# The fourth group of pooled sums in a hybrid decoder step, in five pieces between the issues of value pages

## Chip, cores and metric

The kernel runs on one core of a Trainium2 chip. The metric is the device time of one launch in microseconds (us). A core has a matrix engine (TensorE, PE in the rows; its weight loads are PEld), a vector engine (VectorE, DVE), a scalar engine (ScalarE, ACT), GpSimd (POOL) and a fifth (SyncE, SP) that only issues transfers. Each works through its own list of instructions in order, and they meet by semaphores. An engine's sequencer is marked with a q (POOLq).

## What is computed

Two layers of a decoder trunk, over 256 prompt tokens and 8 sequences of 8 sample tokens (320 columns). Each layer mixes by three kinds of heads, then runs a gated feed-forward part:

```python
h   = rms_norm(x, norm1[l]);  proj = h @ w_in[l]
q, k, v, z, xbc, dt_raw, xp = jnp.split(proj, SPLITS, axis=-1)
o_sb   = stick_breaking_attention(q, k_all, v_all, ...)   # sample tokens read 2048 cached positions, in pages of 128
y_ssd  = ...                                              # chunked state-space scan, 16 heads, and new states
y_pool = multiscale_pool(xp, pool_hist, ...)
x = x + jnp.concatenate([o_sb, y_ssd, y_pool], axis=-1) @ w_out[l]
x = x + (jax.nn.silu(g_c) * u) @ w_down[l]

def multiscale_pool(...):                                 # 4 groups of 128 channels, windows 2, 4, 8, 16
    for g, win in enumerate(POOL_WINDOWS):
        wsum = sum of the last `win` rows of group g
        pooled.append(wsum / count)
    diff = pooled - xp
    y = einsum('blgc,gcd->blgd', diff, pool_w) * pool_scale
```

## The kernel before

Channels lie on partitions, tokens along the free axis. The large products (w_in, w_out, w_gate, w_up, w_down) stream weights in units, split each into a high and a low part and run three matmuls for each tile; they fill most of the time. Between w_in and w_out of each layer lies the **mix stage**, about 320 to 615 us after the start in layer 0 and about 1965 to 2255 us in layer 1. All that changes lies there.

The mix stage is written out by hand as 152 **slots**, numbered 8*qn + k. Every engine has its own loop over the slots, and does in each what belongs to it. In slot s TensorE transposes a page of cached keys (`key_page`, L1332), multiplies a page of cached values by attention weights (`value_page`, L1376, from slot 16 on), in some slots computes scores of a half chunk (`chunk_z`, L1344), and then does the step that the table `MIX` names for the slot: ("pool", g) is the product of group g's pooled difference with pool_w (L1473; groups 0 to 3 in slots 27, 28, 29 and 39), ("c", blk, j) are sums for the scan (L1421; for block 1 in slots 30 to 33), ("n", h) is a part of the new prompt state (L1453; slots 34 and 36) which reads the tile `xw`.

Value pages lie in a ring of 8 (`vring`). GpSimd issues them: in slot s, from 16 on, `value_in` waits until TensorE has used the page that lies in place s mod 8, reads the page's number into a register (L582, a TENSOR_LOAD and two register operations), computes an address (L583, MOVE) and issues the transfer (L583, DMA_DIRECT2D, 256 KB). The page issued in slot s is the one that TensorE needs in slot s + 8. The first eight pages are issued ahead of slot 0.

Behind the issue of its slot GpSimd does other work, also in order: `pooled(g)` for groups 0 to 3 in slots 1, 6, 9 and 20; `gate(blk)` in slots 18 and 41 (L641 to L645, with two drains); `weighted_x(blk)`, which writes `xw` (L616), in slots 5, 28 and 46. `pooled(g)` adds a row of sums to itself, shifted, g + 1 times (L595), so that the window doubles each time, from `xp` into `p1`, from `p1` into `p2` and back; behind each sum stands `pool.drain()` (L596), which holds GpSimd's sequencer until what it issued is done. Then come the means and differences (L599 to L608, drains L602 and L606), and the last of them releases TensorE's ("pool", g) through `p_diff`. ("n", 0) waits for `xw` of block 1 through `blk_xw`.

Of the kernel before, what the change touches and what calls it, by code (L numbers as in the profile page):

```python
# [20 lines left out]
ALU = mybir.AluOpType  # L21
# [31 lines left out]
WINS = (2, 4, 8, 16)  # L53
# [73 lines left out]
def build(nc, a, o):  # L127

    with ExitStack() as ctx:
# [11 lines left out]
        def sb(name, shape, dt=F32):  # L141
            off = at[0]
            at[0] += (size(shape) + 31) // 32 * 32
            return sb_at(name, shape, dt, off)
# [49 lines left out]
        XPL = SEQ + PH + NB * (NT + PH)  # L194
        xp = sb("xp", [P, PLT, XPL])
# [212 lines left out]
        def read(eng, l, *step):  # L408

            b, n = USE[step]  # L410
            eng.wait_ge(mix_read[b], l * USES[b] + (n + 1))
# [119 lines left out]
        def _(pool):  # L531
# [30 lines left out]
            for l in range(DEPTH):  # L562
# [14 lines left out]
                def value_in(q, k):  # L577

                    if q:
                        pool.wait_ge(v_used, l * (CHUNKS * 8) + (8 * (q - 1) + k + 1))  # L580
                    at_page = (q // 4 * 2 + k // 4) * PAGES + 4 * (3 - q % 4) + k % 4
                    page = pool.value_load(pages[0:1, at_page:at_page + 1], min_val=0, max_val=a["cache_v"].shape[1] - 1)  # L582
                    pool.dma_start(vring[:, k, :], a["cache_v"][l, page].rearrange("s h d -> s (h d)")  # L583
                                   ).then_inc(v_loaded[k], 16)

                xps = xp[:, :, SEQ + PH:].rearrange("p g (b t) -> p g b t", b=NB)

                def pooled(g):

                    win = WINS[g]  # L590
                    src, w, bufs = xp[:, g, :], 1, [p1, p2]
                    while w < win:
                        dst = bufs[0][:]
                        bufs.reverse()
                        pool.tensor_tensor(dst[:, 2 * w - 1:], src[:, 2 * w - 1:], src[:, w - 1:XPL - w], ALU.add)  # L595
                        pool.drain()  # L596
                        src, w = dst, 2 * w
                    news = pdiff[:, g, SEQ:TOK].rearrange("p (b t) -> p b t", b=NB)
                    pool.tensor_scalar(pdiff[:, g, 0:SEQ], src[:, PH:PH + SEQ], 1.0 / win, None, ALU.mult)  # L599
                    pool.tensor_scalar(news, src[:, SEQ + PH:].rearrange("p (b t) -> p b t", b=NB)[:, :, PH:], 1.0 / win,  # L600
                                       None, ALU.mult)
                    pool.drain()  # L602

                    pool.tensor_tensor(pdiff[:, g, 0:16], src[:, PH:PH + 16], con[:, K_CNT + 16 * g:K_CNT + 16 * g + 16],
                                       ALU.mult)
                    pool.drain()  # L606
                    pool.tensor_tensor(pdiff[:, g, 0:SEQ], pdiff[:, g, 0:SEQ], xp[:, g, PH:PH + SEQ], ALU.subtract)
                    pool.tensor_tensor(news, news, xps[:, g, :, PH:], ALU.subtract).then_inc(p_diff, 1)  # L608

                def weighted_x(blk):  # L610

                    T = tokens(blk)[1]
                    pool.wait_ge(blk_exp, l * 3 + blk + 1)
                    if blk == 0:
                        read(pool, l, "dec")
                    pool.tensor_tensor(xw[0:T, :].rearrange("p (h d) -> p h d", h=SSH),  # L616
                                       xtok[0:T, 0:SSW].rearrange("p (h d) -> p h d", h=SSH),
                                       tk[0:T, 3, :].unsqueeze(2).broadcast_to([T, SSH, DH]), ALU.mult
                                       ).then_inc(blk_xw, 1)

                def conv_tails_out():
                    read(pool, l, "ctail", 1)
                    read(pool, l, "ctail", 2)
                    pool.dma_start(o["new_ssm_conv_prompt"][l, 0], ctail[0:3, :]).then_inc(conv_stored, 16)
                    pool.dma_start(o["new_ssm_conv_sample"][l].rearrange("b k c -> (b k) c"), ctail[3:27, :]
                                   ).then_inc(conv_stored, 16)
                    pool.dma_start(poolw[:], a["pool_w"][l].rearrange("g c d -> c g d")).then_inc(poolw_loaded, 16)

                def pool_tails_out():
                    read(pool, l, "ptail", 0)  # L630
                    read(pool, l, "ptail", 1)
                    pool.dma_start(o["new_pool_prompt"][l, 0], ptailP[:]).then_inc(tail_stored, 16)
                    pool.dma_start(o["new_pool_sample"][l].rearrange("b k c -> (b k) c"), ptail[0:NB * PH, :]
                                   ).then_inc(tail_stored, 16)

                def gate(blk):

                    cols = slice(blk * P, (blk + 1) * P)
                    read(pool, l, "y", blk, 2)
                    read(pool, l, "y", blk, 3)  # L640
                    pool.tensor_tensor(y[:, :, cols], y[:, :, cols], z[:, :, cols], ALU.mult)  # L641
                    pool.drain()
                    pool.tensor_tensor(z[:, :, cols], y[:, :, cols], y[:, :, cols], ALU.mult)
                    pool.drain()
                    pool.tensor_tensor(z[:, 0:4, cols], z[:, 0:4, cols], z[:, 4:8, cols], ALU.add).then_inc(y_sq, 1)  # L645

                def state_decay(i):

                    s_old = s_seq[i % 4]
                    written(pool, l, "T", i, 0)  # L650
                    written(pool, l, "T", i, 1)
                    pool.tensor_tensor(s_old[:], s_old[:], dec[:, :, 2 + i:3 + i].broadcast_to([P, SST, NS]), ALU.mult
                                       ).then_inc(s_decayed, 1)

                def state_rows(i):

                    if i >= 2:
                        written(pool, l, "N", i - 2, 1)
                    elif i == 0:
                        written(pool, l, "y", 2, 3)  # L660
                    pool.tensor_scalar(bm[:, i % 2, :], xtok[0:SAMP, SSW:], con[0:SAMP, K_SEQ + i:K_SEQ + i + 1], None,
                                       ALU.mult).then_inc(s_bm, 1)

                def state_out(i):
                    read(pool, l, "N", i, 0)
                    read(pool, l, "N", i, 1)
                    pool.dma_start(o["new_ssm_sample"][l, i].rearrange("(j e) p n -> (e p) j n", e=2), s_seq[i % 4][:]
                                   ).then_inc(s_stored[i % 4], 16)
# [5 lines left out]
                for qn in range(CHUNKS + 3):  # L674
                    for k in range(8):
                        slot = 8 * qn + k
                        if 2 <= qn <= CHUNKS:
                            value_in(qn - 1, k)
                        if slot in (1, 6, 9, 20):
                            pooled((1, 6, 9, 20).index(slot))  # L680
                        for blk in range(3):
                            if slot == SLOT["cum", blk] + 2:
                                weighted_x(blk)
                        if slot == SLOT["ctail", 2] + 1:
                            conv_tails_out()
                        if slot == SLOT["ptail", 1] + 1:
                            pool_tails_out()
                        for blk in range(2):
                            if slot == SLOT["y", blk, 3] + 1:
                                gate(blk)  # L690
                        if slot == SLOT["n", 1] + 1:
                            read(pool, l, "n", 0)
                            read(pool, l, "n", 1)
                            pool.dma_start(o["new_ssm_prompt"][l, 0].rearrange("(j e) p n -> (e p) j n", e=2), snew[:]
                                           ).then_inc(snew_stored, 16)
                        for i in range(NB):
                            if slot == SLOT["N", i, 1] + 1:
                                state_out(i)
                            if slot == SLOT["T", i, 1] + 1:
                                state_rows(i)  # L700
                                state_decay(i)
# [29 lines left out]
                n = KT // 2 if l + 1 < DEPTH else KT // 2 - 1  # L731
# [352 lines left out]
        def _(pe):  # L1084
            def products(l, base, n, planes, half=8, between=None, ready=None, side=None, swap=0,
# [38 lines left out]
                if n > 1:  # L1124
                    with pe.Fori(1 if between else 0, n) as i:
                        one(i + base)

            DOWN = [down for _, down in B_PART]
            def norm_sum(n):

# [1193 lines left out]
```

## Time and profile before

| | |
|---|---|
| time, median of 3 runs (lowest, highest) | 3336.67 us (3335.12, 3338.84) |
| the profiled execution: its time, its span | 3336.89 us, 3334.1 us |
| busy: PE, PEld, DVE, ACT, POOL | 96%, 91%, 57%, 40%, 12% of the span |
| mean granted clock of TensorE | 0.982 of full speed |
| chain that ended last, by engine | PE 90%, issue 2%, ACT 2%, POOLq 2%, POOL 1%, DMA 1%, DVE 1% |

The span is that of the traced instructions, from the first to the last; the execution's own time is 2.8 us longer. "Chain that ended last" follows the program back from its last instruction, at each step to what released it. "issue" is time in which an engine waited for nothing that the profile shows. The idle time of an engine counts only where the chain goes through it.

### The profile page before, as it was taken

The page shows a single profiled execution, that of the slowest core. Times are in us where ns is not written, and L with a number is a line of the kernel's source. Part 1 is how long each engine was busy: PE and PEld are TensorE (multiplying, and loading weights), DVE is VectorE, ACT ScalarE, POOL GpSimd, SP SyncE. Part 2 cuts the span into 40 slices and gives each one's busy share as a digit, 9 for nine tenths or more (in the row PEclk, how much of TensorE's full clock was granted, in tenths as well). Part 3 has the DMA queues.
Part 4 walks back from the last instruction along what each step waited for, and adds up shares of the span by engine and source line. Part 5 has one row for each costly group of instructions (what it writes and reads, how often), then busy time and mean ns, then how long its engine had stood idle before and what let it go on. Part 6 is the DMA issues. An engine that isn't in the chain of part 4 may idle for free.

```text
span 3334.1 us, 62446 instructions
## 1 busy us (share of the span) xinstructions
PE 3217.1 (96%) x23776; PEld 3025.9 (91%) x23776; DVE 1902.7 (57%) x3339; ACT 1348.0 (40%) x1663; POOL 408.7 (12%) x513
## 2 busy tenths in 40 slices
PE   7999899899999999999999998989999999999998
PEld 7999566699999999999999985658999999999998
DVE  4574655466653666456656655454666546654664
ACT  4553555434433333333335545563444333333332
POOL 0000654220000000000200025531100000000002
PEclk9999898899999999999999999999999999999999
DMA  6443698644444444444444447985444444444443
GB/s 186 139 127 107 213 304 282 219 151 151 147 145 151 149 146 148 151 156 142 150 143 130 135 132 227 322 288 172 150 151 149 143 151 151 144 149 150 151 145 103
DMA packets 469098, 554.37 MB, mean 166 GB/s; under 512 B 20635, under 2 KB 414444, under 8 KB 468788
## 3 DMA queue, kind: packets, MB, share of 16 engines
q1 hardware_dynamic: 440275, 466.93, 44.1%
q0 software_dynamic: 26192, 84.73, 7.9%
q8 instruction: 114, 1.87, 0.2%
q10 hardware_dynamic: 2449, 0.27, 0.1%
q14 instruction: 68, 0.56, 0.1%
HBM read 535.50 MB, written 16.38 MB: 166 GB/s over the span
## 4 chain that ended last, share of the span: by engine, by line
PE 90%; issue 2%; ACT 2%; POOLq 2%; POOL 1%; DMA 1%; DVE 1%; ACTq 0%; DVEq 0%
PE ps L1107 26%; PE ps L1108 26%; PE ps L1109 26%; PE ps L1332 2%; PE ps L1376 2%; PE ps L1344 1%; PE ps L1494 1%; PE ps L1484 1%; POOLq L596 1%; DMA vring<-in_cache_v 1%; PE ps L1478 1%; POOLq L582 0%; PE ps L1421 0%; ACT wz L934 0%; PE ps L1358 0%
## 5 line engine op out<-in xcount | busy, mean ns | idle before, releaser
L1579 DVE TENSOR_TENSOR wl<-raw,wh 128x1024 fp32r<-128x1024 f32 (+1 forms) x752 | 924.6, 1239 | 1027.2 <-ACT wh L746 1020.4
L746 ACT ACTIVATE wh<-raw 128x1024 fp32r<-128x1024 f32 (+1 forms) x752 | 781.5, 1041 | 1637.4 <-PE ps L1109 1635.0
L1107 PE MATMUL ps<-fh,wh 128*128 128x320 f32 x2816 | 870.6, 309 | 0.0
L1109 PE MATMUL ps<-fh,wl 128*128 128x320 f32 x2816 | 870.1, 309 | 0.0
L1108 PE MATMUL ps<-fl,wh 128*128 128x320 f32 x2816 | 870.1, 309 | 0.0
L1107 PEld LDWEIGHTS ps<-fh,wh 128*128 128x128 f32 x2816 | 528.5, 188 | 0.2
L1108 PEld LDWEIGHTS ps<-fl,wh 128*128 128x128 f32 x2816 | 528.5, 188 | 0.2
L1109 PEld LDWEIGHTS ps<-fh,wl 128*128 128x128 f32 x2816 | 528.5, 188 | 0.0
L1107 PE MATMUL ps<-hh,wh 128*128 128x320 f32 x1408 | 438.4, 311 | 5.5 <-DVE wl L1579 4.5
L1107 PE MATMUL ps<-ah,wh 128*128 128x320 f32 x1408 | 437.1, 310 | 0.0
L1109 PE MATMUL ps<-hh,wl 128*128 128x320 f32 x1408 | 436.2, 310 | 0.0
L1109 PE MATMUL ps<-ah,wl 128*128 128x320 f32 x1408 | 435.1, 309 | 0.0
L1108 PE MATMUL ps<-hl,wh 128*128 128x320 f32 x1344 | 416.4, 310 | 0.0
L1108 PE MATMUL ps<-al,wh 128*128 128x320 f32 x1344 | 415.2, 309 | 0.0
L1107 PEld LDWEIGHTS ps<-hh,wh 128*128 128x128 f32 x1408 | 265.4, 188 | 7.6 <-issue 5.0
L1107 PEld LDWEIGHTS ps<-ah,wh 128*128 128x128 f32 x1408 | 264.3, 188 | 1.6 <-issue 0.3
L1109 PEld LDWEIGHTS ps<-hh,wl 128*128 128x128 f32 x1408 | 265.3, 188 | 0.0
L1109 PEld LDWEIGHTS ps<-ah,wl 128*128 128x128 f32 x1408 | 264.3, 188 | 0.0
L1108 PEld LDWEIGHTS ps<-hl,wh 128*128 128x128 f32 x1344 | 253.3, 188 | 0.0
L1108 PEld LDWEIGHTS ps<-al,wh 128*128 128x128 f32 x1344 | 252.3, 188 | 0.0
L722 POOL DMA_DIRECT2D out_new_ffn_conv_prompt<-ftail x6 | 3.1, 523 | 1612.0 <-DVE ftail L1671 1612.0
L1332 PE MATMUL ps<-con,kring 128*128 128x128 f32 x1024 | 167.9, 288 | 7.6 <-ACT kT L910 6.9
(355 smaller groups left out, 3572.1 us busy)
## 6 DMA issues: line engine op xcount, KB each, us to landing
raw<-in_w_gate SPq DMA_DIRECT2D x88, 1024.0 KB, 5.1
raw<-in_w_up SPq DMA_DIRECT2D x88, 1024.0 KB, 5.1
raw<-in_w_in SPq DMA_DIRECT2D x72, 1024.0 KB, 5.2
kring<-in_cache_k SPq DMA_DIRECT2D x256, 256.0 KB, 4.0
vring<-in_cache_v POOLq DMA_DIRECT2D x256, 256.0 KB, 4.6
raw<-in_w_down SPq DMA_DIRECT2D x64, 1024.0 KB, 5.4
raw<-in_w_out SPq DMA_DIRECT2D x32, 1024.0 KB, 5.5
raw<-in_w_down SPq DMA_DIRECT2D x32, 768.0 KB, 4.6
```

Source lines behind the costliest of these rows:

```text
L596: pool.drain()
L746: act.activation(wh[:, s % 2, half, :], raw[:, s, half, :], ACT.Copy).then_inc(hi_done, 1)
L1107: pe.matmul(out, wh[:, s % 2, kk, w], hi(row), start=first, stop=False)
L1108: pe.matmul(out, wh[:, s % 2, kk, w], lo(row), start=False, stop=False)
L1109: mm = pe.matmul(out, wl[:, s % 2, kk, w], hi(row), start=False, stop=last)
L1332: mm = pe.transpose(ps[4 + n % 2][:, j * P:(j + 1) * P], kring[:, k, j * P:(j + 1) * P], ident)
L1344: mm = pe.matmul(ps[q % 2][32 * j:32 * j + 32, :], qp[:, q // 4, bb, j, :], kT[bb][:, j, :], start=(bb == 0), stop=(bb == 1))
L1376: mm = pe.matmul(ps[6][32 * j:32 * j + 32, 0:P], wz[:, k // 4, k % 4, j, :], vring[:, k, j * P:(j + 1) * P], start=False, stop=last)
L1478: mm = pe.transpose(bank[:, j * P:(j + 1) * P], s_seq[i % 4][:, 4 * h + j, :], ident)
L1484: mm = pe.matmul(bank[:, j * 16:(j + 1) * 16].rearrange("p (e t) -> p e t", e=2), sT[:, i % 2, j * P:(j + 1) * P], csS[:, 2 * j:2 * j + 2, ...
L1494: mm = pe.matmul(bank[:, j * NS:(j + 1) * NS], xw[0:SAMP, (4 * h + j) * P:(4 * h + j + 1) * P], bm[:, i % 2, h * NS:(h + 1) * NS], start=T ...
L1579: dve.tensor_tensor(wl[:, s % 2, half, :], raw[:, s, half, :], wh[:, s % 2, half, :].bitcast(F32), ALU.subtract).then_inc(lo_done, 1)
```

## The change

The function `pooled(g)` is taken apart into `pooled_sum(g, n)`, one doubling with its drain, and `pooled_mean(g)`, the rest. Groups 0 to 2 are still made in one go in slots 1, 6 and 9. Group 3, which was made whole in slot 20, is now made in five pieces: its four sums in slots 22, 23, 24 and 25 and its mean in slot 26, each behind the issue of that slot's value page.

```diff
-                def pooled(g):
-                    win = WINS[g]
-                    src, w, bufs = xp[:, g, :], 1, [p1, p2]
-                    while w < win:
-                        dst = bufs[0][:]
-                        bufs.reverse()
-                        pool.tensor_tensor(dst[:, 2 * w - 1:], src[:, 2 * w - 1:], src[:, w - 1:XPL - w], ALU.add)
-                        pool.drain()
-                        src, w = dst, 2 * w
+                def pooled_sum(g, n):
+                    w = 2 ** n
+                    src = (p2, p1)[n % 2][:] if n else xp[:, g, :]
+                    dst = (p1, p2)[n % 2][:]
+                    pool.tensor_tensor(dst[:, 2 * w - 1:], src[:, 2 * w - 1:], src[:, w - 1:XPL - w], ALU.add)
+                    pool.drain()
+
+                def pooled_mean(g):
+                    win, src = WINS[g], (p1, p2)[g % 2][:]
...
                        if 2 <= qn <= CHUNKS:
                            value_in(qn - 1, k)
-                        if slot in (1, 6, 9, 20):
-                            pooled((1, 6, 9, 20).index(slot))
+                        for g, at_ in enumerate((1, 6, 9)):
+                            if slot == at_:
+                                for n in range(g + 1):
+                                    pooled_sum(g, n)
+                                pooled_mean(g)
+                        if 22 <= slot < 26:
+                            pooled_sum(3, slot - 22)
+                        if slot == 26:
+                            pooled_mean(3)
```

The lists of TensorE, VectorE, ScalarE and SyncE stay as they were. On GpSimd, in layer 0, this stood around slot 20 before; the first row is the issue of slot 20's page, the last one begins that of slot 21's (`pages` holds the page numbers, `p_0_150` and `p_0_151` are `p1` and `p2`; drains are not listed, and stand where the code has them):

```order
L583 DMA vring<-in_cache_v 128x512
L595 TENSOR_TENSOR p_0_150<-xp 128x454
L595 TENSOR_TENSOR p_0_151<-p_0_150 128x452
L595 TENSOR_TENSOR p_0_150<-p_0_151 128x448
L595 TENSOR_TENSOR p_0_151<-p_0_150 128x440
L599 TENSOR_SCALAR pdiff_152<-p_0_151 128x256
L600 TENSOR_SCALAR pdiff_152<-p_0_151 128x64
L604 TENSOR_TENSOR pdiff_152<-p_0_151,con 128x16
L607 TENSOR_TENSOR pdiff_152<-pdiff_152,xp 128x256
L608 TENSOR_TENSOR pdiff_152<-pdiff_152,xp 128x64
L582 TENSOR_LOAD pages
```

The nine compute instructions have left this place, and the issue of slot 21 follows that of slot 20 at once. In the changed kernel this stands in slots 22 to 24, from the issue of slot 22's page to that of slot 24's (the sum is on line 593 there):

```order
L583 DMA vring<-in_cache_v 128x512
L593 TENSOR_TENSOR p_0_150<-xp 128x454
L582 TENSOR_LOAD pages
L582 ISA x2
L583 ISA
L583 DMA vring<-in_cache_v 128x512
L593 TENSOR_TENSOR p_0_151<-p_0_150 128x452
L582 TENSOR_LOAD pages
L582 ISA x2
L583 ISA
L583 DMA vring<-in_cache_v 128x512
```

Each sum, and the drain behind it, now stands between two issues. Behind slot 26 the mean ends like this, with the issues of slots 27 and 28 and then the tile `xw` (`xw_134`, line 617 there):

```order
L608 TENSOR_TENSOR pdiff_152<-pdiff_152,xp 128x256
L609 TENSOR_TENSOR pdiff_152<-pdiff_152,xp 128x64
L582 TENSOR_LOAD pages
L582 ISA x2
L583 ISA
L583 DMA vring<-in_cache_v 128x512
L582 TENSOR_LOAD pages
L582 ISA x2
L583 ISA
L583 DMA vring<-in_cache_v 128x512
L617 TENSOR_TENSOR xw_134<-xtok,tk 128x1024
```

Before, the issues of eight pages (slots 21 to 28) stood between the group's last instruction and `xw`; now two do. The number of instructions and of drains (six for the group) is the same.

## Rows read from the trace of the kernel before

**Rows 1.** TensorE in order of time, layer 0: start, us, engine, line, operation, tiles

```profile
382.26 0.81 PE L1473 MATMUL ps<-pdiff,poolw 128*128 128x320 f32 x2
382.91 0.60 PE L1332 MATMUL ps<-con,kring 128*128 128x128 f32 x4
392.24 0.66 PE L1376 MATMUL ps<-vring,wz 128*32 128x128 f32 x8 [8.73 <-DMA vring<-in_cache_v]
392.67 1.94 PE L1344 MATMUL ps<-kT,qp 128*32 128x512 f32 x8
394.53 1.22 PE L1473 MATMUL ps<-pdiff,poolw 128*128 128x320 f32 x2
...
396.11 0.43 PE L1376 MATMUL ps<-vring,wz 128*32 128x128 f32 x8
...
402.86 1.04 PE L1344 MATMUL ps<-kT,qp 128*32 128x512 f32 x8
...
405.36 0.43 PE L1376 MATMUL ps<-vring,wz 128*32 128x128 f32 x8
405.71 1.16 PE L1453 MATMUL ps<-xtok,xw 128*128 128x128 f32 x8
```

**Rows 2.** The same view in layer 1, the same slot

```profile
2036.53 0.66 PE L1376 MATMUL ps<-vring,wz 128*32 128x128 f32 x8 [8.61 <-DMA vring<-in_cache_v]
```

**Rows 3.** GpSimd in order of time, layer 0, slots 20 to 28; brackets: idle before

```profile
378.14 0.55 POOL L583 DMA_DIRECT2D vring<-in_cache_v  x1 [0.59 <-issue]
378.70 0.95 POOL L595 TENSOR_TENSOR p<-xp 128x454 f32<-128x454 f32 x1
382.08 3.27 POOL L595 TENSOR_TENSOR p<-p 128x452 f32<-128x452 f32 x3 [2.43 <-issue]
385.52 1.57 POOL L599 TENSOR_SCALAR pdiff<-p 128x256 f32<-128x256 f32 x1 [0.17 <-issue]
...
388.04 0.72 POOL L607 TENSOR_TENSOR pdiff<-pdiff,xp 128x256 f32<-128x256 f32 x1
...
389.25 0.59 POOL L583 DMA_DIRECT2D vring<-in_cache_v  x1 [0.21 <-issue]
390.42 0.54 POOL L583 DMA_DIRECT2D vring<-in_cache_v  x1 [0.57 <-issue]
...
397.69 0.54 POOL L583 DMA_DIRECT2D vring<-in_cache_v  x1 [0.62 <-issue]
398.24 1.92 POOL L616 TENSOR_TENSOR xw<-xtok,tk 128x1024 f32<-128x1024 f32 x1
```

**Rows 4.** Busy us by engine in stretches (PE, PEld, DVE, ACT, POOL), granted clock, DMA

```profile
383.00:392.00 9.00, 0.51 (x5) 0.27 (x3) 3.09 (x4) 1.01 (x3) 6.79 (x11) 0.62 0.32 91
392.00:396.00 4.00, 3.76 (x22) 1.69 (x22) 0.00 (x0) 0.22 (x1) 1.71 (x4) 0.58 0.75 213
```

**Rows 5.** The drain behind the first sum at 378.14: its ns (min/median/max), its start

```profile
L596 POOLq DRAIN  x1: 3854/3854/3854, 378.1 to 378.1; - x1
```

**Rows 6.** GpSimd in order of time: other work that follows a drain close behind an issue

```profile
344.60 1.33 POOL L599 TENSOR_SCALAR pdiff<-p 128x256 f32<-128x256 f32 x1 [3.16 <-issue]
...
422.27 0.54 POOL L583 DMA_DIRECT2D vring<-in_cache_v  x1 [1.46 <-issue]
...
427.47 1.89 POOL L643 TENSOR_TENSOR z<-y 128x1024 f32<-128x1024 f32 x1 [2.27 <-issue]
...
2026.50 3.27 POOL L595 TENSOR_TENSOR p<-p 128x452 f32<-128x452 f32 x3 [2.85 <-issue]
...
2071.93 1.89 POOL L643 TENSOR_TENSOR z<-y 128x1024 f32<-128x1024 f32 x1 [1.97 <-issue]
```

**Rows 7.** Page transfers: count, KB, median us to landing; page at 378.14, then 389 to 398

```profile
vring<-in_cache_v POOLq DMA_DIRECT2D x1, 256.0 KB, 3.7
...
vring<-in_cache_v POOLq DMA_DIRECT2D x8, 256.0 KB, 3.2
```

**Rows 8.** The means' first instruction over the whole run: ns, min/median/max

```profile
L599 POOL TENSOR_SCALAR pdiff<-p x8: 847/856/2078, 344.6 to 2029.9; 128x256 f32<-128x256 f32 x8
```

## The prediction, on record before the changed kernel ran

> **What bounds the kernel now.** I read the page first: TensorE is busy nearly all the time, and the chain that ended last gives GpSimd's sequencer and GpSimd itself a few per cent. So the change can only matter where the chain leaves TensorE inside the mix stage. I asked TensorE's own order of time there, looking for brackets. One wait stands out: it was ready for slot 29's value page at 383.51 (392.24 less 8.73) and waited 8.73 us for a transfer [rows 1]; layer 1 shows the same wait of 8.61 us at the same slot [rows 2]. Then GpSimd's order of time: slot 20's page was issued at 378.14, then all of group 3 ran, and slot 21's page, which is the one that slot 29 needs, went out at 389.25 [rows 3]; it landed some 3 us later. The wait is therefore GpSimd's delay of the issue, 11.1 us from one issue to the next where two issues that follow at once are 1.17 apart (389.25 to 390.42).
>
> Behind the wait TensorE ran slowly for a while: the granted clock was 0.62 and 0.58 in these stretches [rows 4], on its way to the lower of its levels, 1.2 instead of 2.4 GHz. The same three steps took 0.66, 1.94 and 1.22 us where they take 0.43, 1.04 and 0.81 otherwise [rows 1]: 1.54 us lost. The spot costs about 8.7 + 1.5 = 10.2 us a layer, 20 us in the run. That is the most the change can win.
>
> **What the change does, part by part.**
>
> *Removed: the block in slot 20.* Slot 21's page goes out at 378.14 + 1.17 = 379.31, lands by 382.5, and slot 29 starts at 383.5 without a wait. Slot 22's page goes out at 380.48. With its clock kept, TensorE would reach slot 30 at 383.5 + (396.11 - 392.24) - 1.54 = 385.8, that is 10.28 us ahead of before, and everything behind it by as much if nothing new is late: ("n", 0) of slot 34, at 405.71 before [rows 1], at 395.43.
>
> *Added: a drain behind each of five issues.* This is the term that decides. The same number of drains runs, but before only the first of them stood right behind an issue. Its length was 3854 ns [rows 5] for a sum of 0.95 us: the sum ended at 379.65, and the next one could start only 2.43 us later; the three sums behind it, with no new issue between, took 3.27 us together, no gap worth counting [rows 3]. Wherever a drain follows an issue this gap is there: 3.16, 2.27, 2.85 and 1.97 us [rows 6]; in the order of time I found no case without it, and 0.1 to 0.2 us where no transfer had been issued since the last drain. The drain at 378.14 ended at 382.0 and the page issued at 378.14 landed 3.7 us after issue [rows 7], at 381.9, so my reading is that the drain also waits for the transfer that GpSimd has just issued. So the extra is paid once a block before, and five times now.
>
> The size for each. The two long brackets (3.16, and 2.43 and 2.85 in this very place) follow pages issued 1.2 us apart; 2.27 and 1.97 follow pages about 2 us apart (422.27 with 1.46 idle before it) [rows 6], which is closer to the new order. I take 2.85 for the piece in slot 22, which follows four issues in a row, and 2.1 for the other four. From the end of a drain to the next issue 1.2 us pass (388.04 to 389.25: register load, address, issue) [rows 3]. So:
> - slot 22: issue 380.48; 0.56 (issue) + 0.95 (sum) + 2.85 + 1.2 = 5.56: slot 23's issue at 386.04.
> - slots 23, 24, 25: 0.56 + 0.95 + 2.1 + 1.2 = 4.81 each: slot 26's issue at 400.47.
> - slot 26: the mean from L599 to the next issue took 389.25 - 385.52 = 3.73 us, of which L599 had 1.57 where its median is 0.86 [rows 3, 8]; TensorE's neighbours are quieter now, so 3.73 - 0.71 = 3.02. With issue and gap 0.56 + 3.02 + 2.0 (0.1 of the gap is in the 3.02 already) = 5.58: slot 27 at 406.05, slot 28 at 407.22.
> - `xw` behind it: 407.22 + 0.55 + 1.92 [rows 3] = 409.69.
>
> *TensorE against this.* Slot 34's value page is that of slot 26: issued at 400.47, landed some 3.1 us later [rows 7] at 403.6, where TensorE would want it at 405.36 - 10.28 = 395.1. So 8.5 us of waits lie on the value pages of slots 31 to 34, about 2 us each. Then ("n", 0), which had 5.5 us to spare before (`xw` ended at 400.16, TensorE came at 405.71 [rows 1, 3]), is reached at 403.9 and waits 5.8 us for `xw`. Sum 14.3 for 10.28 saved: ("n", 0) starts 4.0 us later than before. VectorE and ScalarE wait for TensorE here, so nothing hides it, and behind slot 34 the pages are ahead again (GpSimd issues one in 1.17 us, TensorE needs one in about 2). In this tangle of waits its clock will fall again in part; I charge half of the 1.54: 0.7 us, where 0 and 1.54 are the bounds. Sum 4.7 us a layer, less 0.2 for VectorE and ScalarE having run ahead: 4.5, twice 9.0.
>
> Made against the profiled execution, 3336.9 us (its span of 3334.1 and 2.8 around it; 0.2 above the median of the runs): 3336.9 + 9.0 = 3346 us.
>
> **Bounds of the unknown.** The gap at 3.16 throughout gives 4 x 1.06 + 0.31 = 4.6 us more a layer and full clock loss 0.8: 10 a layer, 3357. If a drain only waits for the landing of one lone page, 2.9 to 3.2 us after issue [rows 2, 3, 7] and no more, the gap is about 1.5 for the sums and 1.2 for the mean, and the layer comes out 4.0 - 1.3 - 3 x 0.6 - 0.9 = 0.0, with clock 0 to 1: 3337 to 3339. The Trainium skill, "DMA: Bandwidth & Descriptors", section "Anatomy of one DMA", gives a transfer by GpSimd as 2.0 us + bytes / 436 GB/s, an estimate of 2.6 us for a page; by that alone the pieces would come still closer, and the time would be about 3335. The rows show 3.2 and 3.7, so the page's figure is low here, under the load of the key pages.
>
> **Rivals.**
> - *Pieces fit between the issues* (the other side). If the gap belonged to the first drain after the long gate of slot 18, or to a train of issues, and not to each issue, a slot with a piece takes 0.56 + 0.95 + 0.1 + 1.2 = 2.8 us: slot 26's issue at 391.7, `xw` done at 391.7 + 3.7 + 1.2 + 2.5 = 399.1; no page is late by more than a few tenths, ("n", 0) starts at 399.1 instead of 405.7. 6.6 us a layer, and no clock lost: 3323 us. It decides from a mean gap of about 1.35 us downwards: there the new order starts to win. For it speaks only that no drain of before stood behind one lone issue after a pause of 5 us; against it all brackets of [rows 3, 6], whose smallest is 1.97. 9 in 100.
> - *Landing is all that counts*: as worked out in the bounds, 3337 to 3343, no measurable change. For it: the drain of [rows 5] ended 0.1 us behind the landing. Against it: at 422.27 the multiplication of 2.38 us covers most of the landing and still 2.27 were left. 22 in 100.
> - *Forecast*: gap near 2.1 to 2.9, slower. 69 in 100.
>
> **How the numbers follow.** Within 0.2% (6.7 us, about what a measurement of this kernel can tell from no change) is 3330 to 3343.3. The forecast's own range is 3342 to 3355; with the landing rival it begins at 3338, and the 9 in 100 of the fitting pieces and a few above stay out. Slower by over 0.2%: 0.69. Same: 0.22. Faster: 0.09.
>
> **What would show each step.** In the changed kernel's GpSimd order: slots 22 to 26 issued 4.5 to 5.6 us apart, each drain there 3.4 to 4.3 us long, against 2.8 us apart under the first rival. In TensorE's: no wait at slot 29; brackets of 1 to 3 us on the value pages of slots 31 to 34; a wait of 5 to 6 us at ("n", 0) that is put down to GpSimd's `xw`; a granted clock below 1 somewhere between 388 and 412. If `xw` ends before 405.7 the forecast is wrong in its sign; if the pieces are 4.8 us apart and the time still doesn't rise, then ("n", 0) was not where it binds, and I have missed work that hides it.

## The result and the profile after

The changed kernel takes 3343.03 us (median of 10 runs, 3336.82 to 3348.22); the kernel before, run beside it on the same chip, 3335.0 us (10 runs, 3329.73 to 3339.55). The ratio is 1.0022 with an interval of 1.0012 to 1.0032: slower, by 4 to 11 us. The profiled execution took 3342.78 us, its span 3340.4 us, its mean granted clock is 0.980. Line numbers of the kernel after are 8 higher than before on TensorE.

TensorE in layer 0, the kernel after, in order of time (answers to [rows 1]); brackets are idle time and what ended it:

```profile
382.98 0.43 PE L1384 MATMUL ps<-vring,wz 128*32 128x128 f32 x8
385.36 0.43 PE L1384 MATMUL ps<-vring,wz 128*32 128x128 f32 x8
...
387.80 0.42 PE L1384 MATMUL ps<-vring,wz 128*32 128x128 f32 x8 [0.48 <-DMA vring<-in_cache_v]
388.76 1.16 PE L1429 MATMUL ps<-con,tk 128*128 128x128 f32 x8 [0.54 <-DVE pool_lo L2066]
...
392.41 0.43 PE L1384 MATMUL ps<-vring,wz 128*32 128x128 f32 x8 [1.61 <-DMA vring<-in_cache_v]
...
396.63 0.43 PE L1384 MATMUL ps<-vring,wz 128*32 128x128 f32 x8 [2.28 <-DMA vring<-in_cache_v]
396.88 1.47 PE L1352 MATMUL ps<-kT,qp 128*32 128x512 f32 x8
398.28 2.08 PE L1429 MATMUL ps<-con,tk 128*128 128x128 f32 x8
...
401.27 0.42 PE L1384 MATMUL ps<-vring,wz 128*32 128x128 f32 x8 [0.22 <-DMA vring<-in_cache_v]
406.92 2.05 PE L1461 MATMUL ps<-xtok,xw 128*128 128x128 f32 x8 [5.22 <-POOL xw L617]
```

The 8.73 us at slot 29 are gone (382.98 has no bracket). In their place stand four short waits on the value pages of slots 31 to 34, 4.59 us together, 0.54 us for VectorE between them, and 5.22 us at ("n", 0), which are put down to GpSimd's `xw`. The same in layer 1 (answers to [rows 2]); slot 33 lies between with 0.79 us:

```profile
2033.78 0.43 PE L1384 MATMUL ps<-vring,wz 128*32 128x128 f32 x8 [1.16 <-DMA vring<-in_cache_v]
2038.10 0.65 PE L1384 MATMUL ps<-vring,wz 128*32 128x128 f32 x8 [0.55 <-DMA vring<-in_cache_v]
...
2047.28 0.42 PE L1384 MATMUL ps<-vring,wz 128*32 128x128 f32 x8 [0.39 <-DMA vring<-in_cache_v]
2053.01 2.04 PE L1461 MATMUL ps<-xtok,xw 128*128 128x128 f32 x8 [5.31 <-POOL xw L617]
```

GpSimd after, layer 0, slots 19 to 28 (answers to [rows 3]):

```profile
375.06 0.58 POOL L583 DMA_DIRECT2D vring<-in_cache_v  x1
...
378.54 0.54 POOL L583 DMA_DIRECT2D vring<-in_cache_v  x1 [0.62 <-issue]
379.09 0.95 POOL L593 TENSOR_TENSOR p<-xp 128x454 f32<-128x454 f32 x1
384.82 0.55 POOL L583 DMA_DIRECT2D vring<-in_cache_v  x1 [4.77 <-issue]
385.38 0.95 POOL L593 TENSOR_TENSOR p<-p 128x452 f32<-128x452 f32 x1
389.06 0.54 POOL L583 DMA_DIRECT2D vring<-in_cache_v  x1 [2.73 <-PE ps L1384]
...
393.56 0.55 POOL L583 DMA_DIRECT2D vring<-in_cache_v  x1 [3.00 <-PE ps L1384]
...
398.21 0.54 POOL L583 DMA_DIRECT2D vring<-in_cache_v  x1 [2.95 <-issue]
...
404.30 0.54 POOL L583 DMA_DIRECT2D vring<-in_cache_v  x1 [0.60 <-issue]
404.86 1.91 POOL L617 TENSOR_TENSOR xw<-xtok,tk 128x1024 f32<-128x1024 f32 x1
```

The issues of slots 22 to 26 stand 6.28, 4.24, 4.50 and 4.65 us apart, and slot 27's follows 4.91 us later (layer 1: 6.58, 4.31, 4.20, 4.39 and 5.58). "<-PE ps L1384" names the semaphore event that came last, TensorE's release of a place in the ring. That release isn't the cause: the place that slot 24's page goes into was free since TensorE's slot 24, before 378, and the issue came at 389.06. GpSimd was held by its drain. The drains show it, one by one (their ns, min/median/max, and start; answers to [rows 5]; the fifth is the first one of the mean):

```profile
L594 POOLq DRAIN  x1: 5052/5052/5052, 378.6 to 378.6; - x1
L594 POOLq DRAIN  x1: 3016/3016/3016, 384.8 to 384.8; - x1
L594 POOLq DRAIN  x1: 3276/3276/3276, 389.1 to 389.1; - x1
L594 POOLq DRAIN  x1: 3097/3097/3097, 393.6 to 393.6; - x1
L603 POOLq DRAIN  x1: 3039/3039/3039, 398.3 to 398.3; - x1
```

And the pages issued at 378.54, 384.82 and 389.06, right ahead of the first three (median us from issue to landing; answers to [rows 7]; those of 393.56 and 398.21 took 3.0 each):

```profile
vring<-in_cache_v POOLq DMA_DIRECT2D x1, 256.0 KB, 4.8
vring<-in_cache_v POOLq DMA_DIRECT2D x1, 256.0 KB, 2.9
vring<-in_cache_v POOLq DMA_DIRECT2D x1, 256.0 KB, 3.2
```

384.82 + 2.9 = 387.7, and the drain ended at 384.8 + 3.0 = 387.8; 378.54 + 4.8 = 383.3, and the drain ended at 378.6 + 5.05 = 383.7. Each of these drains ends with the landing of the page ahead of it, 0.1 to 0.4 us behind.

TensorE's clock (answers to [rows 4]; columns as there):

```profile
396.00:401.00 5.00, 4.37 (x28) 2.91 (x28) 1.06 (x3) 0.44 (x1) 1.75 (x3) 0.66 0.45 111
401.00:407.00 6.00, 0.56 (x10) 0.27 (x9) 1.30 (x3) 5.36 (x10) 4.83 (x7) 0.77 0.47 131
407.00:411.00 4.00, 4.00 (x26) 3.28 (x28) 1.99 (x6) 0.00 (x0) 2.42 (x5) 0.50 0.63 217
```

It fell twice, in the stretch behind the waits of slots 32 and 33, and to the lower level behind the wait at ("n", 0): that step took 2.05 us for the 1.16 of [rows 1].

To measure the whole place free of the rest of the program I take the time from TensorE's cum product in slot 26 to the one in slot 44. Before, in layer 0:

```profile
377.30 0.40 PE L1413 MATMUL ps<-tk,con 128*128 128x16 f32 x2
...
425.97 0.28 PE L1413 MATMUL ps<-tk,con 64*64 64x16 f32 x2
```

That is 48.67 us (layer 1: 48.0). After it is 50.58 (378.22 to 428.80) and 50.81 (2023.71 to 2074.52): 1.91 and 2.82 us longer, 4.7 together. Call this the **cost of the place**. It rests on one trace of each kernel: e4 below has the code of before in all these slots, and in its trace the place took 47.75 and 47.41 us, 1.5 us less in all. So differences of 1 to 2 us in this measure tell nothing.

### The profile page after: what moved, and what is told of

Read it like the earlier page. It is cut to its first block, busy times and chain, and to the rows that moved or that the text cites. A ratio compares the mean times of both kernels' runs of the same rounds, so it can differ in the third digit from the quotient of the medians.

```text
span 3340.4 us, 62446 instructions
## 1 busy us (share of the span) xinstructions
PE 3223.8 (97%) x23776; PEld 3033.6 (91%) x23776; DVE 1901.4 (57%) x3339; ACT 1347.7 (40%) x1663; POOL 408.7 (12%) x513
## 4 chain that ended last, share of the span: by engine, by line
PE 91%; issue 2%; ACT 2%; DVE 2%; POOLq 1%; POOL 0%; ACTq 0%; DVEq 0%; DMA 0%
PE ps L1115 26%; PE ps L1116 26%; PE ps L1117 26%; PE ps L1340 2%; PE ps L1384 2%; PE ps L1352 1%; PE ps L1502 1%; PE ps L1492 1%; PE ps L1486 1%; PE ps L1366 0%; PE ps L1429 0%; ACT wz L942 0%; PE ps L1250 0%; DVE sq L1978 0%; PE ps L1158 0%
```

## The experiments

Ten kernels ran in three groups, each group beside the kernel before. "Cost of the place" is against the trace of before, layer 0 + layer 1; negative is faster. "By ratio" is (ratio - 1) times 3335 us, with its interval.

| kernel | cost of the place, us | ratio | by ratio, us |
|---|---|---|---|
| the change | 1.9 + 2.8 = 4.7 | 1.0022 (1.0012, 1.0032) | 7 (4, 11) |
| e1, pieces with semaphores | -10.2 - 9.6 = -19.8 | 0.994 (0.9924, 0.9957) | -20 (-25, -14) |
| e2, block in slot 22 | -1.9 - 2.8 = -4.7 | 0.9983 (0.9972, 0.9994) | -6 (-9, -2) |
| e3, one more drain in slot 27 | 5.2 + 5.6 = 10.8 | 1.0042 (1.0027, 1.0056) | 14 (9, 19) |
| e4, before, drains only behind the place | -0.9 - 0.6 = -1.5 | 1.0064 (1.0048, 1.008) | 21 (16, 27) |
| e5, block in slot 30 | -9.4 - 5.4 = -14.8 | 0.9964 (0.995, 0.9977) | -12 (-17, -8) |
| e6, before, block with semaphores | -3.7 - 3.8 = -7.5 | 0.9986 (0.9972, 0.9999) | -5 (-9, 0) |
| e7, pieces in slots 30 to 34 | -2.3 + 3.0 = 0.7 | 1.0005 (0.9992, 1.0019) | 2 (-3, 6) |
| e8, drains of the sums doubled | 2.0 + 1.6 = 3.6 | 1.0027 (1.0014, 1.004) | 9 (5, 13) |
| e9, no drain in the whole mix stage | -8.4 - 7.5 = -15.9 | 0.9957 (0.9943, 0.9971) | -14 (-19, -10) |
| e10, `xw` ahead of the mean | 1.0 + 0.9 = 1.9 | 1.0014 (1.0, 1.0027) | 5 (0, 9) |

**e1: the same five pieces, without drains.** The changed kernel with each step chained to the next by a semaphore.

```diff
-                    pool.tensor_tensor(dst[:, 2 * w - 1:], src[:, 2 * w - 1:], src[:, w - 1:XPL - w], ALU.add)
-                    pool.drain()
+                        if n:
+                            pool.wait_ge(p_sum, l * 7 + n)
+                        pool.tensor_tensor(dst[:, 2 * w - 1:], src[:, 2 * w - 1:], src[:, w - 1:XPL - w], ALU.add
+                                           ).then_inc(p_sum, 1)
```

> The changed kernel, with group 3's pieces in the same slots 22 to 26, but chained by a semaphore (each sum counts it up, the next piece waits for it) instead of by drains; nothing is left out. Theory (a drain also waits for the page that GpSimd has just issued, 2 to 3 us beyond the sum): without drains the slots with a piece are 1.7 to 2 us apart (0.55 issue, 0.95 sum, 0.2), not 4.2 to 6.3; no page is late, xw is ready before TensorE comes to (n, 0), the wait of 8.7 us at slot 29 is gone and nothing takes its place: about 10 us a layer, ratio to before 0.994 (3315 us). Rival (work of any kind behind each issue is what costs, whatever closes it): spacing stays over 4 us and the time at 1.002 of before.

Measured: 0.994, as expected, 27 us below the change. GpSimd in order of time, slots 22 to 24 (the issues go on at 381.70 and 383.33):

```profile
377.38 0.54 POOL L584 DMA_DIRECT2D vring<-in_cache_v  x1 [0.61 <-issue]
377.93 0.96 POOL L621 TENSOR_TENSOR p<-xp 128x454 f32<-128x454 f32 x1
378.81 0.55 POOL L584 DMA_DIRECT2D vring<-in_cache_v  x1
379.38 0.95 POOL L621 TENSOR_TENSOR p<-p 128x452 f32<-128x452 f32 x1
380.26 0.55 POOL L584 DMA_DIRECT2D vring<-in_cache_v  x1
```

The first three sums take 1.44 us of GpSimd each with their issue, barely more than the 1.17 of an issue alone; the next page's issue follows the sum without a gap, so its register load and address are worked off while the sum runs. `xw` ends at 390.6, and TensorE has two waits left up to slot 34, 0.97 for VectorE and 0.91 for ScalarE. So the pieces, their slots and their arithmetic are not what costs. The drains are.

**e2: the whole group in slot 22.** The change's code undone, the block of before moved by two slots.

```diff
-                        if slot in (1, 6, 9, 20):
-                            pooled((1, 6, 9, 20).index(slot))
+                        if slot in (1, 6, 9, 22):
+                            pooled((1, 6, 9, 22).index(slot))
```

> The kernel before with one number changed: the whole of group 3 in slot 22 instead of 20, with its drains. Theory (each drain close behind an issue pays 2 to 3 us, so the number of such drains counts): one such drain as before, so the block takes 10.6 us; page 23 goes out some 11 us after page 22, TensorE waits about 7 us at slot 31 instead of 8.7 at slot 29, xw is in time. Ratio 0.999 to 1.000, 1 to 4 us faster than before. Rival (the place costs: work in slots 22 to 26 stands too close ahead of xw): as slow as the change, ratio 1.002, with a wait of several us at (n, 0).

Measured: 0.9983, a little better than expected. GpSimd spends 11.9 us from slot 22's issue to slot 23's, and TensorE has one wait for it, at slot 31 (6.96 us in layer 1):

```profile
393.67 0.65 PE L1376 MATMUL ps<-vring,wz 128*32 128x128 f32 x8 [6.49 <-DMA vring<-in_cache_v]
```

and not at ("n", 0), since `xw` ends at 399.3. So the later slots are not what costs. In one go the group pays for one landing there and wins 5 to 6 us on before; in five goes it pays for five and loses 5 to 7.

**e3: one drain more.** The change, and a bare drain behind slot 27's issue, with nothing to wait for but that page.

```diff
+                        if slot == 27:
+                            pool.drain()
```

> The changed kernel with one bare drain more in each layer, behind the issue of slot 27's page, with no compute instruction ahead of it in that slot. Theory: the drain waits until that page has landed, 3.0 to 3.3 us from the issue; slot 28's issue and xw come 3.1 us later, (n, 0) too: 6 us more than the change, ratio to before about 1.004. Rival (the extra belongs to a drain behind a compute instruction, not to the transfer): under 0.1 us a drain, ratio as of the change, 1.002.

Measured: 1.0042. The added drain of layer 0 (ns, start) and what TensorE waits for `xw` now, where it waited 5.22:

```profile
L690 POOLq DRAIN  x1: 3290/3290/3290, 403.5 to 403.5; - x1
```

```profile
410.63 0.77 PE L1463 MATMUL ps<-xtok,xw 128*128 128x128 f32 x2 [8.54 <-POOL xw L617]
```

The last step of the mean ended at 403.55, so no GpSimd work was under way, and the drain lasted 3.29 us; its page landed 3.2 us after issue. All of it comes out at ("n", 0): 8.54 - 5.22 = 3.32 us. The price of a drain behind a fresh page is measured by itself here, and it reaches the time in full (3.3 and 2.8 us of the place, by layer).

**e4: bare drains where I thought there was cover.** The kernel before, with drains in slots 50, 54, 58 and 62.

```diff
+                        if slot in (50, 54, 58, 62):
+                            pool.drain()
```

> The kernel before with a bare drain behind the issues of slots 50, 54, 58 and 62 of each layer, where GpSimd has nothing else to do and is up to 8 slots ahead. It is to measure the drain itself against the landing of the page issued just ahead. Theory: each of the 8 drains lasts 3 to 5 us and ends 0.1 to 0.6 us after the landing; the time stays (ratio 1.000), since the lead covers it. Rival (a drain costs a fixed 2 us after an issue, whenever the page lands): lengths all near 2 us and not in step with the landings.

Measured: 1.0064. A miss on the time, which was to stay at 1.000. The drains ended with the landings as was said, but lasted longer, 3.4 to 6.8 us over both layers, for the pages landed later here. That of slot 58 (its ns and start, and its page's landing in us):

```profile
L682 POOLq DRAIN  x1: 6810/6810/6810, 460.0 to 460.0; - x1
```

```profile
vring<-in_cache_v POOLq DMA_DIRECT2D x1, 256.0 KB, 6.6
```

Behind it in the same slot GpSimd makes the tile `bm`, which TensorE needs in slot 60 for the sample states, and TensorE waits 9.84 us (9.44 in layer 1):

```profile
467.93 2.05 PE L1496 MATMUL ps<-bm,xw 64*128 64x128 f32 x8 [9.84 <-issue]
```

I had looked only at the eight slots of lead that value pages have. A drain holds back all that stands behind it on GpSimd, and the tile with the least lead decides.

**e5: the whole group in slot 30.** The block with its drains, in two tiles of its own, behind `xw` in the program.

```diff
-                        if 22 <= slot < 26:
-                            pooled_sum(3, slot - 22)
-                        if slot == 26:
-                            pooled_mean(3)
+                        if slot == 30:
+                            for n in range(4):
+                                pooled_sum(3, n)
+                            pooled_mean(3)
```

> Group 3 made whole, with its six drains, behind the issue of slot 30's page, in two tiles of its own. Theory (a drain costs the landing of the page issued just before it, once for a block, and what counts is whether TensorE has that much lead over the issues and whether the block stands ahead of xw): GpSimd is some 11 to 12 us in the block; the issues have about 10 us of lead by then and xw of slot 28 is done before it, so TensorE waits at most 2 to 3 us on the page for slot 39 and not at (n, 0); ratio about 0.994 to 0.996 to the kernel before, near the 0.994 of the pieces chained by semaphores. Rival (the number of drains or the place in a page train sets the time wherever the group stands): a wait of 6 to 9 us shows up at slot 38 or 39 and the ratio is 0.998 to 1.000.

Measured: 0.9964. The first drain lasted 5.79 us and slot 31's page went out at 403.05, 13.7 us after slot 30's, longer than expected, and yet TensorE waited for no page behind it, and at most 1 us for anything between slots 30 and 40. TensorE came to slot 39, which needs the page issued at 403.05, at 406.64: one landing, in a block, is covered there. In layer 1 it had 2.19 and 0.52 us of page waits in slots 27 and 28, ahead of the block; they are not its doing.

**e6: the kernel before without the group's drains.** Group 3 whole in slot 20, its steps chained by semaphores as in e1.

> The kernel before, with group 3 whole in slot 20, each of its steps chained to the next by a semaphore instead of a drain. Theory (of the 11.1 us from issue to issue about 2.5 are the first drain waiting for the page's landing, the rest is work): the issues of slots 20 and 21 stand 8 to 8.8 us apart, TensorE's wait at slot 29 shrinks from 8.7 to 5.5 to 6.5 us, ratio 0.998 to 0.999. Rival (the wait comes from the block being in slot 20 at all, the drains only mark work that takes as long anyway): 11 us apart, wait 8.7, ratio 1.000.

Measured: 0.9986, the theory's value, though its interval reaches 0.9999. The block, issue to issue, and the wait that it leaves:

```profile
376.07 0.55 POOL L584 DMA_DIRECT2D vring<-in_cache_v  x1 [0.59 <-issue]
376.63 0.95 POOL L620 TENSOR_TENSOR p<-xp 128x454 f32<-128x454 f32 x1
377.67 3.14 POOL L620 TENSOR_TENSOR p<-p 128x452 f32<-128x452 f32 x3
...
383.72 0.59 POOL L584 DMA_DIRECT2D vring<-in_cache_v  x1
```

```profile
387.25 0.65 PE L1405 MATMUL ps<-vring,wz 128*32 128x128 f32 x8 [4.90 <-DMA vring<-in_cache_v]
```

7.65 us for the 11.1 of before: the gap of 2.43 us behind the first sum [rows 3] is 0.09, and 1.1 us more is saved on other steps. Of that, 0.7 us is the mean's first instruction, which took 0.85 us here and 1.57 in the trace of before, and isn't shown to be the drains' doing. Expected were 8 to 8.8 and a wait of 5.5 to 6.5; it is 4.90 and 4.47, which is 3.8 and 4.1 less than before. So the one drain behind the fresh page accounts for 2.3 us of the wait, and more than half of the wait was the work standing all in one slot.

**e7: the five pieces in slots 30 to 34.** As e5, but in pieces with their drains.

> The five pieces with their drains in slots 30 to 34 (two tiles of their own), behind xw instead of ahead of it. Theory (each piece costs its page's landing wherever it stands, and the price shows at the first thing TensorE needs of GpSimd): issues 4.2 to 4.8 us apart again, group 3 done some 22 us after the issue of slot 30's page; now the product of group 3 in slot 39 waits for it, 6 to 9 us, and there is no wait at (n, 0). Ratio 0.999 to 1.000, about 12 us above the whole block in slot 30. Rival (the damage of the change came from standing ahead of xw, and later pieces are free): no wait over 2 us, ratio 0.996 like the whole block there.

Measured: 1.0005, and 14 us above e5. The issues stand 4.3 to 6.0 us apart once more, and the wait is where group 3 is first needed:

```profile
414.23 1.41 PE L1486 MATMUL ps<-pdiff,poolw 128*128 128x320 f32 x2 [6.23 <-POOL pdiff L614]
```

(9.67 us in layer 1.) Later slots don't make the pieces cheap. Each pays its landing there too.

**e8: the drains of the sums doubled.**

```diff
                         if 22 <= slot < 26:
                             pooled_sum(3, slot - 22)
+                            pool.drain()
```

> The changed kernel with a second drain right behind the drain of each of the four sums. Theory (a drain waits for the landing of what GpSimd issued, and has nothing left to wait for the second time): second drains of under 0.1 us, issues 4.2 to 6.3 us apart as in the changed kernel, ratio 1.002. Rival (each drain costs a fixed couple of us in this neighbourhood): 2 us more a slot, waits of 8 us more a layer, ratio 1.007 or more.

Measured: 1.0027, the change's within the intervals. The eight added drains:

```profile
L687 POOLq DRAIN  x8: 41/41/41, 383.5 to 2041.0; - x8
```

41 ns each. A drain costs next to nothing by itself; what costs is the issue between one and the next.

**e9: no drain at all in the mix stage.** e1, with semaphores also in groups 0 to 2 and in the gates.

> Pieces in slots 22 to 26 as in the change, with semaphores in place of every drain of GpSimd in the mix stage, those of groups 0 to 2 and of the gates too. Theory (only drains behind a fresh page whose page TensorE then waits for cost anything, and those of group 3 were the only such): same as with group 3's alone chained, 0.994, or up to 3 us better (0.993). Rival (drains of the other groups and gates cost too): another 5 us or more, ratio 0.992 or below.

Measured: 0.9957, no better than e1, whose interval it overlaps. The rival's 0.992 or below lies outside its interval: it falls. Whether the other drains cost a little stays open, since e9 has a loss of its own. TensorE waits 2.21 and 2.32 us for VectorE's `pool_lo` at the step of slot 31 (0.97 us in layer 0 of e1) and runs slower behind it. Ahead of that `pool_lo` VectorE's scan took 2.52 us for 1.28 in e1:

```profile
386.11 2.52 DVE L1980 TENSOR_TENSOR_SCAN sq<-rz,sq,lq 128x512 f32<-128x512 f32 x1
```

GpSimd, earlier here, was computing `xw` at the same time (385.62 to 387.54). Layer 1 shows the same, 2.63 us beside `xw`. That the two hold each other up is a reading of these rows; no run tests it.

**e10: `xw` taken ahead of the mean.** The change, with `weighted_x(1)` in slot 26 ahead of `pooled_mean(3)` (group 3 in tiles of its own).

> The changed kernel, its pieces with their drains in slots 22 to 26, but xw is computed in slot 26 ahead of the mean instead of in slot 28 behind it (group 3 sums in two tiles of its own, since p1 and p2 lie under the tile that TensorE's next step lets be written). Theory (5.2 us of the change's loss stand at (n, 0), which waits for xw): xw ends some 6 us earlier, near 401, and the wait at (n, 0) is gone; slot 27's page goes out 2 us later, so slot 35's value page waits 3 to 4 us instead; net 1 to 2 us a layer and some clock won back, ratio 0.9995 to 1.0015. Rival (xw is not what binds, the issues are): as much waiting behind as was won, ratio 1.002.

Measured: 1.0014, inside the theory's range, though not told apart from the change's 1.0022 by the ratios, so the rival (1.002) isn't excluded. `xw` ends at 401.0, there is no wait at ("n", 0), and slot 35's value page takes its place:

```profile
408.53 0.66 PE L1390 MATMUL ps<-vring,wz 128*32 128x128 f32 x8 [5.07 <-DMA vring<-in_cache_v]
```

(4.17 in layer 1; 3 to 4 were expected.) With 3.8 us of work between slot 26's issue and the first drain of the mean, the step behind that drain started after 0.23 us idle, for 1.30 in the change: work between an issue and the drain covers the landing. But moving `xw` passes most of the lateness on, since GpSimd as a whole is late by then.

## Why the prediction came out as it did

The forecast was slower, 3346 in 3338 to 3355, by drains that wait for a page each; measured were 3343.0. The mechanism is the one that was forecast. The size is less sure: 3343.0 lies just inside the 3343.3 up to which the prediction would have called it no change, while the ratio, 1.0022, lies just outside 0.2%. Point by point:

- *The wait at slot 29 goes, and 10.28 us with it.* Right, and somewhat more. Slot 30's page step begins at 385.36 for 396.11, and slot 26's cum product 0.92 later than before (378.22 for 377.30): 11.7 us won. The prediction missed two brackets: before, the page steps of slots 27 and 28 had waited as well, 0.95 and 0.46 us, for pages that were issued at 376.96 and 378.14, behind the drain in slot 18's gate. Both pages went out ahead of group 3's block, so the change didn't remove these 1.4 us: e4, with the code of before, has a single wait of 0.33 us there.

```profile
379.85 0.43 PE L1376 MATMUL ps<-vring,wz 128*32 128x128 f32 x8 [0.95 <-DMA vring<-in_cache_v]
...
381.91 0.42 PE L1376 MATMUL ps<-vring,wz 128*32 128x128 f32 x8 [0.46 <-DMA vring<-in_cache_v]
```

- *Each drain behind a fresh issue waits for the landing.* Right: shown by the five drains of the change, by e3 (nothing else to wait for), by e1 (no drains, no gaps) and by e8 (second drains 41 ns). One reading against the rival "landing is all that counts" was too quick. At 422.27 the multiplication of 2.38 us was said to cover most of the landing; that page took 4.2 us, so 1.3 of the 2.27 us of gap were landing. About 0.8 us were not, and at 2067.03 (page landed after 3.2 us, drain 4.74 us long) 1.5 us were neither landing nor computing. What such a drain behind slot 41's gate waits for besides is open.
- *The size of the gap, 2.85 and 2.1 us.* Spacings of 5.56, then 4.81 three times, then 5.58 were foreseen; they are 6.28, 4.24, 4.50, 4.65 and 4.91. Sum 25.57 against 24.58, 1.0 us less. The drains were to last 3.4 to 4.3 us; they lasted 5.05 behind the train and 3.0 to 3.3 else. The first piece was under-priced by 0.7, the other four over-priced by 0.4 on average; that the sum came out so close is in part luck, for the two errors work against each other. The second rival's rule, lone pages land in 2.9 to 3.2 us and a drain waits for just that, is the better rule for the lone ones; it erred on the page of slot 22, the last of four in a row, with 4.8. Its sum, 3337 to 3339, came out too low by that page and by the full clock loss. The estimate of 2.6 us for a page by the Trainium skill ("DMA: Bandwidth & Descriptors", "Anatomy of one DMA") is low by 0.3 to 0.6 us for the lone pages of layer 0 here, and by 4 us for the page of slot 58 in e4.
- *When the pieces start.* This is the term that was mis-sized most. Slot 22's issue was put at 380.48 and came at 378.54, 1.9 us earlier in the run and 2.9 earlier against TensorE. I had carried over the time of slot 20's issue from one execution [rows 3]. GpSimd was ahead well before that, in code that is the same in both kernels: slot 18's page went out at 365.18 after and at 367.69 before. The drain in slot 18's gate, behind that page, even took some of this back (6.48 us long for 5.85; it ended at 371.7 for 373.7). Why GpSimd runs earlier in the one execution is open. `xw` was done at 406.8 and not at 409.7, 1.9 us by the start and 1.0 by the spacings. In layer 1, the same sum from slot 20's issue at 2022.14 puts slot 22's at 2024.48; it came at 2024.16, 0.3 us earlier in the run and 1.3 against TensorE.
- *The waits behind.* 8.5 us on value pages and 5.8 at ("n", 0) were foreseen; measured 4.6 and 5.2 in layer 0, 2.9 and 5.3 in layer 1. The place and the kind of each are right. The 8.5 is how late slot 34's page was to be for a TensorE at full clock; counted that way it was 6.7 us late (401.27 for 385.36 + 9.25), mostly by the earlier start. Of these 6.7 some 2 are no waits on pages, since TensorE spent 0.5 us on VectorE and 1.7 on steps at a lower clock in the meantime.
- *The clock.* 0.7 us were charged. In layer 0 ("n", 0) itself began only 0.3 us later than before against slot 26, where 4.0 were forecast, and by slot 44 it was 1.9: the other 1.6 were lost behind it at the lower clock. That is the full clock loss that the prediction had as its upper bound (1.54). In layer 1 it is 1.6 and 2.8. What the lower clock took ahead of ("n", 0) cost nothing, since TensorE would have waited there for `xw` anyway.
- *Sum.* 4.5 us a layer foreseen, 1.9 and 2.8 in the trace. The ratio gives 7 us for the run, and the two places 4.7. Most changed kernels stand 1 to 5 us higher by the ratio than by their place. In part that is the one trace of before: against e4's the change costs 2.8 and 3.4 us, 6.2 together, and every other row of the table moves up by 1.5. The rest lies within the intervals. A single trace can't say more: near the end of layer 1's mix stage, where the code is the same, TensorE waits 3.05 us for a page at 2249.03 before and 2.21 at 2253.82 after.

The rival on the other side, pieces that fit between the issues, put the time at 3323. It is false for pieces with drains. Once the drains are gone it is even exceeded: e1 is at 3314, with pieces of 1.4 us for its 2.8.

Where did the gain go? 11.7 us were won in layer 0 at slot 30. Four more landings than before were paid on GpSimd, at about 3 us each, and they came out as 4.6 us at pages, 0.5 for VectorE, 5.2 at `xw` and 3.2 us at a lower clock (steps of 1.47, 2.08, 0.91, 2.05, 1.06 and 0.66 us for 1.04, 1.16, 0.60, 1.16, 0.60 and 0.43): 13.5 us in all, some 1.9 more than was won.

## What to carry to other kernels

Where GpSimd both issues transfers and computes, as here, a drain on it is a wait for the transfer just issued. Splitting such work between issues multiplies that wait, while with a semaphore from each step to the next the same split wins: 1.0022 with drains, 0.994 without, for the same arithmetic in the same slots. If drains must stay, keep the work in one block behind one issue, where TensorE can do longest without the next one (slot 20, 22, 30: 1.000, 0.9983, 0.9964). And ask for each tile behind the drain, not for the pages alone, how much lead it has.

## What the runs showed of the hardware

- A drain of GpSimd with no compute ahead of it and a page of 256 KB just issued lasted 2.9 and 3.3 us in e3, and 3.4 to 6.8 us in e4; where the page's landing was read beside it, the two agree within 0.4 us. Right behind another drain it took 41 ns.
- That holds for the bare drains and those behind a sum. Behind the gate of slot 41 in the kernel before, the drain ended 0.8 and 1.5 us after both its page and its own computing, and no run shows why.
- Such a page landed after 2.9 to 3.2 us in the change when it was issued alone (3.6 for slot 26's in layer 1). The last of four issued 1.2 us apart took 4.8 there, 4.4 in e2, 4.2 in slot 54 of e4 and 6.6 in slot 58. Beside the last, a transfer of 512 KB for the sample states was under way that took 10.5 us; that it is the reason wasn't tested.
- Chained by semaphores, the register load and the issue of the next page overlap with the sum that is running: 1.44 us from issue to issue with a sum of 0.95 us between, 1.17 without.
